# ScalarE in place of GpSimd for the samples' one-hot values, and a later place for the second output gate

## The chip, the cores and the metric

The kernel runs on one core of one Trainium2 chip. The metric is the device time of one execution in microseconds (us); lower is better. Five engines of the core work side by side, each through its own list of instructions in order, and wait for one another through semaphores: TensorE (PE in the profile, its weight loads PEld), VectorE (DVE), ScalarE (ACT), GpSimd (POOL) and SyncE (SP, which here only starts DMA transfers).

## The reference

One layer of a decoder is computed for a prompt (512 tokens) and for 8 samples of 8 new tokens each, 576 tokens in all, model width 1024. An input projection feeds a convolution branch and a matrix-memory branch (mLSTM, 4 heads of width 256); both are gated and merged, and a feed-forward part follows. What matters here is the memory of the samples, which each head updates as

```
C_new = decay[..., None, None] * C + jnp.einsum('bhs,bhsv,bhsk->bhvk', w_s, vc, kc)
...
mlstm_out = (jax.nn.sigmoid(og.astype(jnp.float32)) * hm).astype(x.dtype)
```

For a sample b, the sum over its own 8 tokens s gives a 256x256 matrix from weighted values and keys. `og` is the output gate of the branch.

## The kernel before, in words

Everything is float32 at nearly full precision: TensorE's fast form of float32 (fp32r) is used on split numbers, a high and a low part, so a projection "unit" (one tile of 128 output rows times 576 tokens) is three products: h_hi with w_hi, h_lo with w_hi, h_hi with w_lo. A unit's 128x1024 weights are loaded into `raw` (two slots), ScalarE copies them into `w_hi` (`split_hi`, line 801, called `hi_of` in a head), and VectorE subtracts to get `w_lo` (`split_lo`, line 1689, called `lo_of`, which afterwards runs some taps of the depthwise convolution, line 1911). TensorE runs a unit only once its `w_lo` is there.

The four heads are four turns of one loop on every engine. A head has 10 units: q, k, v, og, gb, two of each. The weights of unit j+2 are split while unit j or j+1 runs: `hi_of(6)` splits the weights of unit 8, `hi_of(7)` those of unit 9. Behind `hi_of(6)` and `hi_of(7)` ScalarE applies a sigmoid with bias to the finished units 6 and 7 and writes the output gate to `merged` (line 967). On VectorE the matching `lo_of(6)` and `lo_of(7)` stand in front of the evaluation of the head's output.

TensorE's order in the second part of a head is: unit 6 with the products of the old states beside it, a small product read by ScalarE (line 1434), unit 7, then the products PV 0 to PV 4 (lines 1449 to 1456, one for each 128 prompt tokens and one for the samples), the prompt's new state (line 1464, two products "CP"), and then unit 8 with eight sample products beside it, one in front of each eighth of the unit (line 1475, "CS 0" to "CS 7", two matmuls each), and unit 9. These results rotate through four PSUM banks; a product may only start when the one four places before it has been read out. So PV 3 waits until ScalarE has copied PV 0 out of PSUM into `num` (line 972), and CS 4 waits until VectorE has read CS 0 and added it to the old state `cs` (line 2015).

The samples' keys and weighted values are stacked by six small DMAs (line 621) into `stk`, in two groups of four samples, each with 96 rows: high, low and high again parts of 4 samples x 8 tokens. For one sample, the values of the others must be zero. So `wvs` holds eight copies of the value block, each multiplied by the sample's column of `oh96`, which is 1 in that sample's rows and 0 elsewhere. GpSimd makes the copies (line 742): one instruction for each group of four samples, 96x1024 elements. It does this behind the eight subtractions that give the low parts of the old states (line 737) and in front of the stores of the states. TensorE waits for `wvs` in front of CS 0.

VectorE's order behind the PV operands is: `w2_lo` (line 1973), `kvn_lo` (line 1977), `lo_of(6)`, `lo_of(7)`, each with two taps, the samples' outputs (lines 1985 to 1993), statistics and small scalars (lines 1997 to 2011), and then CS 0 to CS 7 (line 2015).

Of the kernel before, what the change touches and what calls it, by code (L numbers as in the profile page):

```python
# [27 lines left out]
F32 = mybir.dt.float32  # L28
F32R = mybir.dt.float32r
ALU = mybir.AluOpType  # L30
ACT = mybir.ActivationFunctionType
# [7 lines left out]
SB, SL = 8, 8  # L39
SG = SB // 2  # L40
GT = SG * SL
RING = 3
NH, HD = 4, 256
# [172 lines left out]
def build(nc, xT, vecs, gate_w, gate_b, cache, w_cgcv, w_head, w_ga, w_co, w_o, w_fi, w_fp, w_fo0, w_fo1, w_fo2,  # L216
          st_c, st_n, st_m, y, conv_p, conv_s, cn_p, m_p, c_s, n_s, m_s):
    with ExitStack() as ctx:  # L218
        place = [-(-nc.sbuf_base // 32) * 32]

        def sb(name, cols, dt=F32, parts=P):
            shape = [parts] + (list(cols) if isinstance(cols, (list, tuple)) else [cols])
            t = nc.alloc_sbuf_tensor_at(name, shape, dt, offset=place[0])
            place[0] += -(-4 * int(np.prod(shape[1:])) // 32) * 32
            return t

        def sem(name):
            return ctx.enter_context(nc.semaphore(name))
# [45 lines left out]
        oh96 = sb("oh96", SG)  # L274
# [33 lines left out]
        wvs = nc.alloc_sbuf_tensor_at("wvs", [P, SB, HD], F32R, offset=head_base + 4 * 2 * T)  # L308
# [37 lines left out]
        stk = nc.alloc_sbuf_tensor_at("stk", [P, 2, 2 * HD], F32R, offset=hf_base + 4 * 2 * T)  # L346
# [70 lines left out]
        def slot(s):  # L417
            return ps[:, 2 * s:2 * s + 2, 0:HALF]

        def bank(k):  # L420
            return ps[:, 4 + k % 4, :]
# [14 lines left out]
        def vcol(c, parts=P):  # L436
            return vec[0:parts, c:c + 1] if isinstance(c, int) else vec[0:parts, bass.ds(c, 1)]
# [50 lines left out]
        stk_placed = [sem(f"samples_kv_stacked{g}") for g in range(2)]  # L488
        kvsplit_ready = sem("samples_kv_split")
        wvs_ready = sem("wvs_ready")  # L490
# [166 lines left out]
        def _(pool):  # L657
# [75 lines left out]
            def states(h, last=False):  # L733

                for b in range(SB):
                    pool.wait_ge(cshi_ready, h * SB + (b + 1))
                    pool.tensor_tensor(cs_lo[:, b % RING, :], cs[:, b, :, :].rearrange("p k v -> p (k v)"),  # L737
                                       cs_hi[:, b % RING, :].bitcast(F32), ALU.subtract).then_inc(cslo_ready, 1)

                for g in range(2):  # L740
                    pool.wait_ge(stk_placed[g], h * 48 + 48)
                    pool.tensor_tensor(wvs[0:3 * GT, g * SG:g * SG + SG, :],
                                       stk[0:3 * GT, g, HD:2 * HD].bitcast(F32).unsqueeze(1)
                                       .broadcast_to([3 * GT, SG, HD]),
                                       oh96[0:3 * GT, :].unsqueeze(2).broadcast_to([3 * GT, SG, HD]), ALU.mult)\
                        .then_inc(wvs_ready, 1)

                pool.wait_ge(act_read, h * ACT_USES + (START + ACT_USES))
                pool.dma_start(cn_p[bass.ds(h, 1)].rearrange("o p k v -> (o p) k v"), cp[:, :, :])\
                    .then_inc(cp_stored, 16)  # L750

                pool.wait_ge(dve_read, h * DVE_USES + (START + 13))
                pool.dma_start(c_s[bass.ds(h, 1)].rearrange("o p b k v -> (o p) b k v"), cs[:, :, :, :])\
                    .then_inc(cs_stored, 16)
                pool.wait_ge(cs_stored, h * 16 + 16)
                pool.wait_ge(cp_stored, h * 16 + 16)
                pool.sem_inc(cp_free, 1)
                if not last:
                    pool.dma_start(cs[:, :, :, :], st_c[bass.ds(h + 1, 1)].rearrange("o p b k v -> (o p) b k v"))\
                        .then_inc(cs_loaded, 16)  # L760
# [31 lines left out]
        def _(act):  # L792
# [113 lines left out]
            with act.Fori(0, NH) as h:  # L906
                def hi_of(j):
                    split_hi(h * (PER_HEAD // 2) + (U_B + j + 2) // 2, j % 2)

                def use(k):  # L910
                    act.wait_ge(attn_ready, h * USES + (k + 1))

                for j in range(2):
                    hi_of(j)
                    evac_bias(h, j, halves(qkv[:, 0, :, :], j))
                hi_of(2)

                act.wait_ge(mdiag_ready, h + 1)

                def gcol(item, parts=P):  # L920
                    return cols[0:parts, item, bass.ds(h, 1)]

                for s in range(NB):
                    act.activation(wts[:, W_OFF[s]:W_OFF[s] + P], mdiag[:, s, :], ACT.Exp, bias=gcol(I_G[s]))\
                        .then_inc(w_ready, 1)
                    for t in range(s + 1, NB):
                        o = W_OFF[s] + (t - s) * P
                        act.activation(wts[:, o:o + P], negm[:, bass.ds(h, 1), t * P:t * P + P]
                                       .rearrange("p o n -> p (o n)"), ACT.Exp,
                                       bias=gcol(OFF[s, t])).then_inc(w_ready, 1)  # L930
                act.activation(wts[0:TS, W_OFF[NB]:W_COLS], msamp[0:TS, :], ACT.Exp, bias=gcol(I_G[NB], TS))\
                    .then_inc(w_ready, 1)
                hi_of(3)
                for j in range(4, 6):
                    hi_of(j)
                    evac_bias(h, j, halves(qkv[:, 2, :, :], j - 4))
                def old_hi(b):

                    if b >= RING:
                        act.wait_ge(old_used, h * SB + (b - RING + 1))  # L940
                    act.activation(cs_hi[:, b % RING, :], cs[:, b, :, :].rearrange("p k v -> p (k v)"), ACT.Copy)\  # L941
                        .then_inc(cshi_ready, 1)

                act.wait_ge(cs_loaded, h * 16 + 16)
                for b in range(RING):
                    old_hi(b)
                for i in range(5):
                    use(T_USE + i)
                    n = P if i < NB else TS
                    act.activation(kvn[0:n, i, 0:2 * HD], bank(T_USE + i)[0:n, :], ACT.Copy).then_inc(act_read, 1)  # L950

                for b in range(RING, SB):
                    old_hi(b)

                use(I_USE)
                act.activation(inter_lo[0:TS, :], bank(I_USE)[TS:P, 0:HD], ACT.Copy)
                act.activation(inter[0:TS, :], bank(I_USE)[0:TS, 0:HD + SB], ACT.Copy).then_inc(act_read, 1)

                act.wait_ge(dve_read, h * DVE_USES + (START + 5))
                act.activation(w2_hi[:, :], wts[:, 0:W_OFF[NB]], ACT.Copy).then_inc(pvhi_ready, 1)  # L960
                act.wait_ge(act_read, h * ACT_USES + (START + 5))
                act.activation(v_hi[:, :, :], kvn[:, 0:NB, HD:2 * HD + 2], ACT.Copy).then_inc(pvhi_ready, 1)
                act.wait_ge(out_stored, 16 * 4)
                for j in range(6, 8):
                    hi_of(j)
                    act.wait_ge(unit_done, h * PER_HEAD + (U_B + j + 1))
                    act.activation(halves(merged, h * 2 + (j - 6)), slot(j % 2), ACT.Sigmoid,
                                   bias=vcol(h * PER_HEAD + (U_B + j))).then_inc(slot_read[j % 2], 1)
                for i in range(5):
                    use(PV_USE + i)  # L970
                    n = P if i < NB else TS
                    act.activation(num[0:n, i, :], bank(PV_USE + i)[0:n, 0:VE], ACT.Copy).then_inc(act_read, 1)
                act.wait_ge(cp_free, h + START)
                for k in range(2):
                    use(CP_USE + k)
                    act.activation(cp[:, k, :], bank(CP_USE + k)[:, 0:VE], ACT.Copy).then_inc(act_read, 1)
                act.wait_ge(hvar_ready, h + 1)
                act.activation(small[:, 2, :], small[:, 1, :], ACT.Sqrt, bias=eps[:, :]).then_inc(hdev_ready, 1)
                for j in range(8, 10):
                    hi_of(j)  # L980
                    act.wait_ge(unit_done, h * PER_HEAD + (U_B + j + 1))
                    act.wait_ge(gb_used, h * 2 + START)
                    act.activation(halves(tmp, j % 2), slot(j % 2), ACT.Sigmoid,
                                   bias=vcol(h * PER_HEAD + (U_B + j))).then_inc(slot_read[j % 2], 1)
# [39 lines left out]
            with act.Fori(0, N_CO // 2) as i:  # L1024
                for p in range(2):
                    for o in range(2):
                        j = i * 4 + (2 * p + o)
# [267 lines left out]
        def _(pe):  # L1295
# [71 lines left out]
            with pe.Fori(0, NH) as h:  # L1367
# [99 lines left out]

                for g in range(2):
                    pe.wait_ge(stk_placed[g], h * 48 + 48)
                pe.wait_ge(wvs_ready, h * 2 + 2)  # L1470

                def state_update(b):
                    use(CS_USE + b)
# [1201 lines left out]
```

## Time and profile before

| | us |
|---|---|
| median of 3 runs | 940.04 (939.7 to 940.3) |
| profiled execution | 938.66 |
| span of that execution, first to last instruction | 937.1 |
| TensorE busy in the span | 922.1 (98%) |
| VectorE busy | 777.3 (83%) |
| ScalarE busy | 460.6 (49%) |
| GpSimd busy | 110.5 (12%) |

The page of the profile gives busy time by engine, the groups of instructions with what they waited for, and the DMA issues. The trace behind it can be asked for waits by engine, for the instructions of one line, and for a timeline: start and duration of each instruction of an engine in a window. A row of a timeline merges neighbours of the same line; its duration is from the start of the first to the end of the last. On one engine the start of an instruction may lie a little ahead of the end that is recorded for the one before it, because they overlap.

### The profile page before, as it was taken

How to read it: one execution, taken by the hardware profiler on the slowest of the kernel's cores; microseconds unless marked ns; L12 is line 12 of the kernel's file. 1: busy time of each engine (PE TensorE's matmuls, PEld its weight loads, DVE VectorE, ACT ScalarE, POOL GpSimd, SP SyncE). 2: the span in 40 equal slices, each digit the busy share in tenths (PEclk: the TensorE clock that was granted, in tenths of full speed). 3: DMA queues.
4: the chain of work that ended last, by engine and by line, in shares of the span. 5: the costliest groups of instructions: out<-in, count | busy, mean ns of one | idle time of the engine just before them, and what ended most of it. 6: DMA issues, size and time to landing. Idle time of an engine off the chain costs nothing. (4 is left out here: it accounts for less than half of the span.)

```text
span 937.1 us, 18353 instructions
## 1 busy us (share of the span) xinstructions
PE 922.1 (98%) x6801; PEld 902.0 (96%) x6801; DVE 777.3 (83%) x1227; ACT 460.6 (49%) x676; POOL 110.5 (12%) x109
## 2 busy tenths in 40 slices
PE   8999999999999999999999999999999999999996
PEld 8999999999999999999999999999999999999995
DVE  6899986989698879976355569999888999989997
ACT  7654442444245334524733345456444555456564
POOL 3011330043006001500231000000000000000001
PEclk9999999999999999999999999999999999999999
DMA  6245225211721452142432232232222223233122
GB/s 220 69 155 193 70 74 226 90 55 63 249 88 40 146 179 90 41 167 70 133 125 81 76 90 69 93 125 99 91 90 92 90 72 110 94 117 105 45 91 101
DMA packets 24123, 100.13 MB, mean 107 GB/s; under 512 B 3312, under 2 KB 6529, under 8 KB 19572
## 3 DMA queue, kind: packets, MB, share of 16 engines
q1 hardware_dynamic: 21240, 78.70, 25.5%
q0 software_dynamic: 1984, 19.72, 5.7%
q10 hardware_dynamic: 832, 0.88, 0.3%
q8 instruction: 34, 0.56, 0.2%
q14 instruction: 33, 0.27, 0.1%
HBM read 85.28 MB, written 12.44 MB: 104 GB/s over the span
## 5 line engine op out<-in xcount | busy, mean ns | idle before, releaser
L1306 PE MATMUL ps<-h_hi,w_hi 128*128 128x288 f32 x896 | 193.6, 298 | 0.0
L1306 PE MATMUL ps<-h_lo,w_hi 128*128 128x288 f32 x896 | 191.5, 296 | 0.0
L1306 PE MATMUL ps<-h_hi,w_lo 128*128 128x288 f32 x896 | 191.2, 295 | 0.0
L801 ACT ACTIVATE w_hi<-raw 128x1024 fp32r<-128x1024 f32 x76 | 80.3, 1057 | 171.5 <-PE ps L1306 168.4
L1306 PEld LDWEIGHTS ps<-h_hi,w_lo 128*128 128x128 f32 x896 | 144.2, 189 | 0.0
L1306 PEld LDWEIGHTS ps<-h_hi,w_hi 128*128 128x128 f32 x896 | 143.4, 189 | 0.8
L1306 PEld LDWEIGHTS ps<-h_lo,w_hi 128*128 128x128 f32 x896 | 144.1, 189 | 0.0
L1689 DVE TENSOR_TENSOR w_lo<-raw,w_hi 128x1024 fp32r<-128x1024 f32 x76 | 101.0, 1329 | 47.1 <-ACT w_hi L801 47.1
L1911 DVE SCALAR_TENSOR_TENSOR conv<-a_p,vec,conv x120 | 97.7, 814 | 1.6 <-DVE conv L1911 1.4
L1566 PE MATMUL ps<-cols_b,late 128*128 128x288 f32 x432 | 62.9, 295 | 0.1
L1566 PE MATMUL ps<-cols_a,main 128*128 128x288 f32 x432 | 62.8, 295 | 0.0
L737 POOL TENSOR_TENSOR cs_lo<-cs,cs_hi 128x512 fp32r<-128x512 f32 x32 | 42.4, 1354 | 156.7 <-ACT cs_hi L941 156.7
L1566 PE MATMUL ps<-cols_b,main 128*128 128x288 f32 x432 | 60.2, 295 | 0.2 <-issue 0.2
L1566 PEld LDWEIGHTS ps<-cols_b,late 128*128 128x128 f32 x432 | 59.0, 188 | 0.3 <-issue 0.3
L1566 PEld LDWEIGHTS ps<-cols_a,main 128*128 128x128 f32 x432 | 59.0, 188 | 0.0
L1566 PEld LDWEIGHTS ps<-cols_b,main 128*128 128x128 f32 x432 | 58.2, 188 | 0.4 <-issue 0.4
L1566 PE MATMUL ps<-hid_a,main 128*128 128x288 f32 x396 | 55.3, 296 | 0.5 <-ACT hf L1104 0.5
L788 POOL TENSOR_TENSOR x<-x,rs 128x288 f32<-128x288 f32 x5 | 3.8, 795 | 429.2 <-ACT rs L1272 429.2
L1566 PEld LDWEIGHTS ps<-hid_a,main 128*128 128x128 f32 x396 | 53.3, 188 | 1.0 <-ACT hf L1104 0.7
L1066 ACT ACTIVATE main<-raw 128x1024 fp32r<-128x1024 f32 (+1 forms) x30 | 31.0, 1032 | 34.8 <-PE ps L1566 17.1
L1071 ACT ACTIVATE main<-main 128x1024 fp32r<-128x1024 f32 (+1 forms) x30 | 31.0, 1033 | 32.2 <-DVE main L2171 32.2
L2171 DVE TENSOR_TENSOR main<-raw 128x1024 f32<-128x1024 f32 (+1 forms) x30 | 35.6, 1186 | 7.5 <-PE ps L1566 7.5
(355 smaller groups left out, 1839.6 us busy)
## 6 DMA issues: line engine op xcount, KB each, us to landing
raw<-w_head_in SPq DMA_DIRECT2D x40, 512.0 KB, 3.5
raw<-w_fp_in SPq DMA_DIRECT2D x18, 1024.0 KB, 4.9
cs<-st_c_in POOLq DMA_DIRECT2D x4, 2048.0 KB, 9.3
c_s_out<-cs POOLq DMA_DIRECT2D x4, 2048.0 KB, 7.4
raw<-w_fo_in SPq DMA_DIRECT2D x8, 1024.0 KB, 4.9
x<-xT_in SPq DMA_DIRECT2D x16, 288.0 KB, 4.2
raw<-w_cgcv_in SPq DMA_DIRECT2D x8, 512.0 KB, 3.6
raw<-w_ga_in SPq DMA_DIRECT2D x8, 512.0 KB, 3.5
```

The lines of the kernel that those rows point to most:

```text
L737: pool.tensor_tensor(cs_lo[:, b % RING, :], cs[:, b, :, :].rearrange("p k v -> p (k v)"), cs_hi[:, b % RING, :].bitcast(F32), ALU.subtract ...
L788: pool.tensor_tensor(x[:, k, at], x[:, k, at], rs[:, at], ALU.mult).then_inc(y_pool_ready, 1)
L801: act.activation(w_hi[:, s, :], raw[:, s, :], ACT.Copy).then_inc(hi_ready, 1)
L1066: act.activation(main[:, 0:4:2, 0, 0:n], blocks_of(i)[:, 1:4:2, :], ACT.Copy).then_inc(a11_a12_hi, 1)
L1071: act.activation(main[:, 1:4:2, 0, 0:n], main_32[:, 1:4:2, 1, 0:n], ACT.Copy).then_inc(s1_s3_hi, 1)
L1306: last = pe.matmul(ps[:, 2 * s + b, 0:HALF], wt[:, w, k * P:k * P + P], src[:, k, b * HALF:b * HALF + HALF], start=(k == 0 and wt is w_hi ...
L1566: last = pe.matmul(ps[:, at, 0:HALF], wrows(rows_, wp)[:, k * P:k * P + P], of(cols_, cp_)[:, k, :], start=(first and k == 0 and wp == 0 a ...
L1689: dve.tensor_tensor(w_lo[:, s, :], raw[:, s, :], w_hi[:, s, :].bitcast(F32), ALU.subtract)\
L1911: steps.on(dve.scalar_tensor_tensor(o, a, wcol, o, ALU.mult, ALU.add))
L2171: dve.tensor_tensor(main_32[:, 1:4:2, 1, 0:n], r[:, 0:2, :], r[:, 2, :].unsqueeze(1).broadcast_to([P, 2, n]), ALU.add).then_inc(s1_s3_sum, 1)
```

## The change

GpSimd's two multiplications per head are taken out. ScalarE makes the eight copies instead, one ACTIVATE Copy for each sample, 96x256, with the column of `oh96` as a per-partition scale. They stand behind the first output gate (unit 6) and in front of the five PSUM copies into `num`. The second output gate (`hi_of(7)`, the wait for unit 7 and its sigmoid) is moved from in front of these PSUM copies to behind them. TensorE's wait counts eight copies per head instead of two. VectorE's program stays as it is.

```diff
-                for g in range(2):
-                    pool.wait_ge(stk_placed[g], h * 48 + 48)
-                    pool.tensor_tensor(wvs[0:3 * GT, g * SG:g * SG + SG, :],
-                                       stk[0:3 * GT, g, HD:2 * HD].bitcast(F32).unsqueeze(1)
-                                       .broadcast_to([3 * GT, SG, HD]),
-                                       oh96[0:3 * GT, :].unsqueeze(2).broadcast_to([3 * GT, SG, HD]), ALU.mult)\
-                        .then_inc(wvs_ready, 1)
...
-                for j in range(6, 8):
+                def og_unit(j):
                     hi_of(j)
                     act.wait_ge(unit_done, h * PER_HEAD + (U_B + j + 1))
                     act.activation(halves(merged, h * 2 + (j - 6)), slot(j % 2), ACT.Sigmoid,
                                    bias=vcol(h * PER_HEAD + (U_B + j))).then_inc(slot_read[j % 2], 1)
+
+                og_unit(6)
+                for b in range(SB):
+                    if b % SG == 0:
+                        act.wait_ge(stk_placed[b // SG], h * 48 + 48)
+                    act.activation(wvs[0:3 * GT, b, :], stk[0:3 * GT, b // SG, HD:2 * HD].bitcast(F32),
+                                   ACT.Copy, scale=oh96[0:3 * GT, b % SG:b % SG + 1]).then_inc(wvs_ready, 1)
                 for i in range(5):
                     use(PV_USE + i)
                     n = P if i < NB else TS
                     act.activation(num[0:n, i, :], bank(PV_USE + i)[0:n, 0:VE], ACT.Copy).then_inc(act_read, 1)
+                og_unit(7)
                 act.wait_ge(cp_free, h + START)
...
-                pe.wait_ge(wvs_ready, h * 2 + 2)
+                pe.wait_ge(wvs_ready, h * SB + SB)
```

## Rows read from the trace of the kernel before

**Rows 1.** The page, busy time of each engine and share of the span.
```profile
PE 922.1 (98%) x6801; PEld 902.0 (96%) x6801; DVE 777.3 (83%) x1227; ACT 460.6 (49%) x676; POOL 110.5 (12%) x109
```

**Rows 2.** Waits of TensorE: line waited for, us in total, times, longest.
```profile
PE ps L1475 <- DVE cs L2015: 1.4, 4, 0.4
```

**Rows 3.** Timeline of TensorE: start, us, line, tiles, idle before it.
```profile
139.28 0.42 PE L1306 MATMUL ps<-h_hi,w_lo 128*128 128x288 f32 x2
140.03 0.51 PE L1475 MATMUL ps<-wvs,stk 96*128 96x256 f32 x2 [0.33 <-DVE cs L2015]
...
228.03 0.39 PE L1475 MATMUL ps<-wvs,stk 96*128 96x256 f32 x1 [0.33 <-DVE cs L2015]
```

**Rows 4.** Timeline of VectorE, head 0, from the PV operands to CS 0.
```profile
124.28 2.92 DVE L1977 TENSOR_TENSOR kvn_lo<-kvn,v_hi 128x1024 fp32r<-128x1024 f32 x1
127.12 2.91 DVE L1689 TENSOR_TENSOR w_lo<-raw,w_hi 128x1024 fp32r<-128x1024 f32 x1
...
131.75 1.22 DVE L1689 TENSOR_TENSOR w_lo<-raw,w_hi 128x1024 fp32r<-128x1024 f32 x1
...
139.23 2.06 DVE L2015 SCALAR_TENSOR_TENSOR cs<-cs,dec,ps 128x512 f32<-128x512 f32 x3
```

**Rows 5.** Timeline of ScalarE, head 0, around the output gates.
```profile
124.77 1.28 ACT L967 ACT_TABLE_LOAD   x1
126.06 0.74 ACT L967 ACTIVATE merged<-ps,vec 128x576 f32 x1
127.53 1.06 ACT L801 ACTIVATE w_hi<-raw 128x1024 fp32r<-128x1024 f32 x1 [0.73 <-PE ps L1306]
128.50 0.72 ACT L967 ACTIVATE merged<-ps,vec 128x576 f32 x1
129.12 1.05 ACT L972 ACTIVATE num<-ps 128x257 f32<-128x257 f32 x3
131.37 0.38 ACT L972 ACTIVATE num<-ps 128x257 f32<-128x257 f32 x1 [1.20 <-PE ps L1453]
131.95 0.38 ACT L972 ACTIVATE num<-ps 64x257 f32<-64x257 f32 x1 [0.19 <-PE ps L1456]
133.88 0.39 ACT L976 ACTIVATE cp<-ps 128x257 f32<-128x257 f32 x1 [1.56 <-PE ps L1464]
```

**Rows 6.** Timeline of TensorE where PV 3 starts, and CS 0.
```profile
129.35 0.28 PE L1451 MATMUL ps<-kvn_lo,wts_hi 128*128 128x256 f32 x1
129.47 0.28 PE L1453 MATMUL ps<-v_hi,wts_lo 128*128 128x258 f32 x1
129.62 0.38 PE L1449 MATMUL ps<-v_hi,wts_hi 128*128 128x258 f32 x1
...
135.24 0.59 PE L1475 MATMUL ps<-wvs,stk 96*128 96x256 f32 x2
```

**Rows 7.** Groups by form (busy us, mean ns of one), and two timelines of neighbours.
```profile
L941 ACT ACTIVATE cs_hi<-cs 128x512 fp32r<-128x512 f32 x32 | 19.3, 627 | 9.8 <-PE ps L1426 9.8
L928 ACT ACTIVATE wts<-negm,cols 128x128 f32 x24 | 8.2, 389 | 0.0
...
87.27 0.97 ACT L928 ACTIVATE wts<-negm,cols 128x128 f32 x3
...
9.67 3.66 ACT L810 ACTIVATE xg_hi<-x,vec 128x576 fp32r<-128x576 f32 x5
```

**Rows 8.** Timeline of GpSimd: the two multiplications of head 0.
```profile
123.14 5.82 POOL L742 TENSOR_TENSOR wvs<-stk,oh 96x1024 fp32r<-96x1024 f32 x2 [4.50 <-DMA stk<-kvs]
```

**Rows 9.** VectorE behind a copy of ScalarE, unit 9 of head 0: both timelines.
```profile
151.64 1.06 ACT L801 ACTIVATE w_hi<-raw 128x1024 fp32r<-128x1024 f32 x1 [4.07 <-PE ps L1306]
...
152.73 1.23 DVE L1689 TENSOR_TENSOR w_lo<-raw,w_hi 128x1024 fp32r<-128x1024 f32 x1 [3.59 <-ACT w_hi L801]
```

**Rows 10.** Stretches: busy us and count by engine, then granted clock of TensorE.
```profile
6.00:8.00 2.00, 1.40 (x13) 1.21 (x11) 0.79 (x2) 1.31 (x4) 1.47 (x9) 1.00 1.03 413
158.00:246.00 88.00, 87.67 (x636) 83.79 (x635) 73.98 (x137) 36.93 (x58) 18.23 (x13) 1.00 0.34 115
```

## The prediction

> **What bounds the kernel now.** I read the page first: TensorE is busy for 98% of the span [rows 1], so a change is worth only what it does to TensorE's gaps. The stretches say the same of the heads: one turn of the loop takes 88.00 us and TensorE is busy for 87.67 of them [rows 10]. Next come TensorE's waits. Within the heads one named wait matters, at line 1475 for VectorE's reading of CS 0, four times, once in each head [rows 2]. Then the timelines, to see how this wait arises and how much slack the neighbours have. The heads repeat within hundredths: CS 4 starts at 140.03 in head 0 and at 228.03 in head 1, 88.00 later [rows 3]. So head 0 is worked out and multiplied by four.
>
> Without any wait CS 4 would follow the two matmuls at 139.28 at the usual pace. Neighbouring matmuls start 0.12 us apart [rows 6], so behind those two it would start at about 139.53; it starts at 140.03 [rows 3]. That is a stall of 0.5 us. It ends just after the first CS reading on VectorE, which starts at 139.23. Three readings take 2.06 us [rows 4], so the first is over at about 139.95 and CS 4 starts less than 0.1 later. VectorE reaches 139.23 without an idle stretch from 124.28 on: no row in this stretch has an idle time before it, and those shown lie end to end [rows 4]. Therefore VectorE's chain already sets CS 4, and whatever delays it by one microsecond delays TensorE by one.
>
> ScalarE sets a second, nearly invisible point. PV 3 starts at 129.62, 0.15 behind the matmul at 129.47 where the pace before was 0.12, and its first matmul takes 0.38 instead of 0.28, as after a short wait [rows 6]. ScalarE's copy of PV 0 starts at 129.12 and ends at 129.50 (a copy of this kind takes 0.38) [rows 5]. So PV 3 has no slack left against this copy: it starts 0.12 after its end.
>
> **The change, part by part.**
>
> GpSimd's part. Two multiplications, 5.82 us per head, go away [rows 8]. TensorE needs `wvs` only at CS 0, at 135.24 [rows 6], and it was there at 128.96; so GpSimd's own time was hidden and its removal gives nothing directly. It gives something to VectorE: while GpSimd multiplies, from 123.14 to 128.96, two subtractions of 128x1024 take 2.92 and 2.91 us, while the same subtraction takes 1.22 at 131.75 with GpSimd idle [rows 4, 8]. VectorE so gains 1.70 + 1.69 = 3.4 us and could be at the end of `lo_of(6)` at about 128.3. What is late next is decided below: the weights it needs then are not there.
>
> Where the copies lie. The first output gate starts at 126.06, takes 0.74 and overlaps its successor by about 0.1, so the first copy can start at 126.70 [rows 5]. Its data are there: GpSimd waited for the stacking DMAs only in front of its first multiplication, and began the second, which needs the second group, at about 126.05 [rows 8]. The wait for `stk` that ScalarE gains costs nothing; queued behind it are the `num` copies, for which TensorE waits.
>
> The price of a copy. No 96x256 copy with a scale column is in the trace, so I build it. A plain copy of 512 elements takes 0.627 us [rows 7], one of 1024 takes 1.06 [rows 5]; one element more costs 0.84 ns. Exponentials of 128 elements with a column operand take 0.389 and follow one another by (0.97 - 0.39)/2 = 0.29 [rows 7]. From them: 0.29 + 128 x 0.84 ns = 0.40 per copy. From the only run of copies with a scale column: 3.66/5 = 0.73 at 576 elements, so 0.73 - 320 x 0.84 ns = 0.46 [rows 7]. The lower end is 0.335, the pace of the plain PSUM copies of 257 elements, (1.05 - 0.38)/2, were the column free [rows 5]; the upper one 0.50, the same with no overlap. I take 0.40, as it comes from the row nearest in size.
> The Trainium skill (ScalarE: Activation LUTs, on what an ACTIVATE costs) states that each column operand adds about 93 ns and that neighbours overlap by as much; by its figures an estimate for 256 elements is 0.40 us, so it speaks for the first of the two rows and against the second, and by it the sum stays as below.
>
> First stall, at PV 3. Eight copies are 3.20 us, so they end in time for the PV 0 copy to start at 126.70 + 3.20 = 129.90. Before, `hi_of(7)` and its gate stood there and it started at 129.12. That is +0.78, and with no slack at PV 3 TensorE waits 0.78 us there. The subtraction `kvn_lo` comes earlier, but this buys nothing: what it frees is in front of PV 3, which ScalarE now sets.
>
> Second stall, at CS 4. The last `num` copy (the samples') follows TensorE and so starts at 131.95 + 0.78 = 132.73 [rows 5]. Now `hi_of(7)` comes: it starts 0.29 later (0.38 less the overlap), at 133.02, and takes 1.06, to 134.08. VectorE picks weights up 0.03 after ScalarE's copy ends (151.64 + 1.06 = 152.70, against 152.73) [rows 9]. So `lo_of(7)` starts at 134.11 instead of 131.75: +2.36. VectorE's program is unchanged, so it stands idle from about 128.3, with everything for CS 0 queued behind this one subtraction. From its start to CS 0 VectorE needs 139.23 - 131.75 = 7.48 us without a gap [rows 4]; CS 0 is read from 141.59, and CS 4 starts at 140.03 + 2.36 = 142.39. Of the 2.36 the first stall holds 0.78, this one the other 1.58 on top of the 0.5 that was there.
>
> The rest is covered. The second gate's sigmoid ends at about 134.7, while the first CP copy may now start at 133.88 + 0.78 = 134.66 [rows 5]: it does not move. Between the two gates no other function is loaded: before, a Copy of weights also lay between them with one table load ahead of both [rows 5], so no load is added. Unit 9's weights are ready at 135.3, ten microseconds ahead. After CS 4 VectorE takes under 0.7 us for each reading (2.06/3) [rows 4] and TensorE a microsecond for each eighth of the unit, so no further wait follows. SyncE's next load into this slot is later by 2.4 us and has the better part of a head to spare. GpSimd's stores wait for ScalarE and VectorE as before.
>
> Sum: 4 x 2.36 = 9.4 us. Nothing in the 98% busy TensorE after the heads can give it back. Against the profiled execution: span 937.1 + 9.4 = 946.5, time 938.66 + 9.4 = 948.1. That execution lies 1.4 below the median of the runs shown; from the median, 940.04 + 9.4 = 949.5. That is the forecast.
>
> **The rivals.**
>
> A: the copies are hidden and only the gate's new place counts. If the pause at PV 3 is no wait, or the copies are quicker than 0.30, the `num` copies stay where they are, and `lo_of(7)` starts at 131.95 + 0.29 + 1.06 + 0.03 = 133.33: +1.58 per head, 6.3 in all, 946.4. Against it stand the 0.12 between copy and PV 3 and the price of a copy.
>
> B: a copy costs more. With 0.46 the PV 0 copy starts at 130.38: +1.26, and with the 1.58 that is 2.84 per head, 951.4. With 0.50 and no overlap it is +1.58 and 3.16 per head, 952.7.
>
> C, the other side: VectorE's relief wins. If `lo_of(7)` had its weights by 131.2, the 3.4 us would wipe out the stall of 0.5 at CS 4 (deciding point: CS 0 read 0.5 earlier than now), 4 x 0.5 = 2.0 us: 938.0. It needs `hi_of(7)` ahead of the last `num` copy, and in the new order it lies behind it, while that copy cannot start before 131.95 since it waits for TensorE [rows 5]. The rule behind this is in the Trainium skill (GPSIMD Engine Reference, Key points): GpSimd shares its SBUF interfaces with VectorE and gets in the way of instructions with two SBUF inputs. The trace agrees, by 2.92 against 1.22; it speaks for the change, and only its gain has nowhere to go.
>
> D: the clock. TensorE waits some 2 us in a stretch at CS 4. If its granted clock fell from 2.4 to 1.2 GHz for the four remaining eighths of unit 8 (4.1 us), each head would lose another 4.1: 966. Against it, the clock stays 1.00 in the start-up stretch where TensorE is busy for only 1.40 of 2 us [rows 10]. The Trainium skill (TensorE: Matmul & The Clock Gate) states that a gate halves the clock of an array that is less busy; no row here shows that in mid-kernel.
>
> E: the change cancels out. The bank of PV 3 and the weights of unit 9 would both have to be ready about as early as now; no row offers that, and the chance stands for a reading of mine that is wrong in both places: within 0.2% of 940.04.
>
> **How the numbers follow.** Forecast 0.70, A 0.11, B 0.12, C 0.02, D 0.02, E 0.03. The forecast's own width (copies from 0.335 to 0.42, starts read to 0.05) is about 947.2 to 950.3. The range takes in A and B whole, so 946.0 to 952.8. About 0.2%, 1.9 us, is what a measurement can tell from no change: slower by more 0.95, within 0.03, faster 0.02.
>
> **What would show it.** In the profile after: GpSimd's line gone and the two subtractions at 1.22; eight copies about 0.40 apart; PV 3 waiting for a `num` copy, about 0.8 per head; an idle stretch of VectorE of about 5.8 us per head in front of `lo_of(7)`, released by ScalarE's `w_hi`; TensorE waiting some 2.1 at CS 4, 8 in all; turns of 90.36 us; clock 1.00. It is wrong if `lo_of(7)` starts less than 1.5 us later than now against its head, or if VectorE's 7.48 us from there to CS 0 shrinks.

## The result and the profile of the changed kernel

The change makes the kernel slower. The median is 952.62 us (951.71 to 954.4, 4 runs) against 939.87 before (939.7 to 940.3, 4 runs); the ratio is 1.0137 with a 95% interval of 1.012 to 1.0155. The profiled execution took 953.48 us with a span of 952.0. On the page of the changed kernel, the busy times, which answer to [rows 1], and the granted clock in 40 slices:

```profile
PE 929.0 (98%) x6801; PEld 908.3 (95%) x6801; DVE 764.6 (80%) x1227; ACT 472.4 (50%) x708; POOL 86.3 (9%) x101
...
PEclk9999999999999999999999999999999999999998
```

GpSimd has lost 24 us, VectorE 13, and TensorE's share is 98% as before: the page alone doesn't show what went wrong. TensorE's waits do (line waited for, us in total, times, longest), beside [rows 2]:

```profile
PE ps L1475 <- DVE cs L2015: 7.6, 4, 1.9
PE ps L1449 <- ACT num L971: 3.1, 4, 0.8
```

These are the two predicted waits, in front of CS 4 and of PV 3, in every head. (The 1.9 is TensorE's idle time by the row; counted from the time at which CS 4 would have started at the usual pace, as the prediction counts, it is 2.1.) In this kernel line 971 is the `num` copy, 966 the value copies, 959 the output gate, 793 the weight copy. The timeline of ScalarE in head 0, beside [rows 5]. The whole head lies 0.58 us later than before, since the start-up of this execution was slower: the row `inter_lo` starts at 121.48 here and at 120.90 before.

```profile
121.48 0.38 ACT L948 ACTIVATE inter_lo<-ps 64x256 f32<-64x256 f32 x1 [4.29 <-PE ps L1434]
...
126.64 0.74 ACT L959 ACTIVATE merged<-ps,vec 128x576 f32 x1
127.28 3.30 ACT L966 ACTIVATE wvs<-stk,oh 96x256 fp32r<-96x256 f32 x8
130.47 0.91 ACT L971 ACTIVATE num<-ps 128x257 f32<-128x257 f32 x3
...
133.29 0.38 ACT L971 ACTIVATE num<-ps 64x257 f32<-64x257 f32 x1 [0.19 <-PE ps L1456]
133.57 1.04 ACT L793 ACTIVATE w_hi<-raw 128x1024 fp32r<-128x1024 f32 x1
```

The eight copies run from 127.28 to the first `num` copy at 130.47, 0.40 us apart. VectorE in the same head, beside [rows 4]:

```profile
124.86 1.22 DVE L1977 TENSOR_TENSOR kvn_lo<-kvn,v_hi 128x1024 fp32r<-128x1024 f32 x1
125.99 1.22 DVE L1689 TENSOR_TENSOR w_lo<-raw,w_hi 128x1024 fp32r<-128x1024 f32 x1
...
134.65 1.23 DVE L1689 TENSOR_TENSOR w_lo<-raw,w_hi 128x1024 fp32r<-128x1024 f32 x1 [5.64 <-ACT w_hi L793]
...
142.14 4.04 DVE L2015 SCALAR_TENSOR_TENSOR cs<-cs,dec,ps 128x512 f32<-128x512 f32 x6
```

Both subtractions take 1.22 instead of 2.92 and 2.91, and VectorE then stands idle for 5.64 us until the weights of unit 9 have been copied. From there to CS 0 it is 142.14 - 134.65 = 7.49 us, as before. On TensorE, head 0 and then heads 1 to 3, beside [rows 3, 6]:

```profile
130.97 0.38 PE L1449 MATMUL ps<-v_hi,wts_hi 128*128 128x258 f32 x1 [0.78 <-ACT num L971]
...
142.94 0.50 PE L1475 MATMUL ps<-wvs,stk 96*128 96x256 f32 x2 [1.90 <-DVE cs L2015]
...
233.28 0.70 PE L1475 MATMUL ps<-wvs,stk 96*128 96x256 f32 x2 [1.90 <-DVE cs L2015]
...
325.13 0.51 PE L1475 MATMUL ps<-wvs,stk 96*128 96x256 f32 x2 [1.90 <-DVE cs L2015]
...
417.03 0.51 PE L1475 MATMUL ps<-wvs,stk 96*128 96x256 f32 x2 [1.90 <-DVE cs L2015]
```

Less the 0.58, CS 4 of head 0 is at 142.36; 142.39 was forecast. From head 0 to head 1 a turn takes 90.34 us, and 90.36 was forecast. But the next two turns take 91.85 and 91.90. The stretches of head 1 show why (us; busy us and count by engine; the eighth number, behind POOL's count, is the granted clock as a share of full speed):

```profile
230.00:232.00 2.00, 1.38 (x11) 1.15 (x9) 1.79 (x11) 0.00 (x0) 0.00 (x0) 1.00 0.09 35
232.00:233.60 1.60, 0.32 (x2) 0.33 (x3) 1.49 (x5) 0.30 (x1) 0.00 (x0) 0.94 0.00 0
233.60:234.00 0.40, 0.40 (x3) 0.40 (x3) 0.40 (x2) 0.00 (x0) 0.00 (x0) 0.50 0.00 0
234.00:236.00 2.00, 2.00 (x10) 2.00 (x10) 1.86 (x4) 0.00 (x0) 0.00 (x0) 0.50 0.00 0
236.00:237.00 1.00, 1.00 (x7) 1.00 (x6) 0.74 (x1) 0.00 (x0) 0.00 (x0) 0.59 0.00 0
237.00:240.00 3.00, 3.00 (x24) 2.82 (x23) 1.63 (x4) 0.78 (x1) 0.05 (x1) 1.00 0.00 0
```

Behind the wait at CS 4 the granted clock falls from 2.4 to 1.2 GHz and is back at about 236.8; from the shares 0.94 and 0.59 it was low from about 233.4, for 3.4 us. The rows of TensorE show it too: a pair of matmuls of unit 8 takes 0.68 us in that time and 0.42 after it.

```profile
233.77 0.68 PE L1306 MATMUL ps<-h_hi,w_hi 128*128 128x288 f32 x2
...
237.22 0.42 PE L1306 MATMUL ps<-h_hi,w_hi 128*128 128x288 f32 x2
```

A turn with such a fall is 91.87 - 90.34 = 1.53 us longer. In this execution heads 1, 2 and 3 have one, head 0 has none.

So the 14.9 us between the two spans are: 0.58 from the start, 4 x 2.34 = 9.4 from the two waits, 3 x 1.53 = 4.6 from the clock, and 0.3 not assigned.

### The profile page after: what moved, and what is told of

The parts are those of the page before. It is cut to its first block and busy times, and to the rows that moved or that the text cites. A ratio compares the mean times of both kernels' runs of the same rounds, so it can differ in the third digit from the quotient of the medians.

```text
span 952.0 us, 18378 instructions
## 1 busy us (share of the span) xinstructions
PE 929.0 (98%) x6801; PEld 908.3 (95%) x6801; DVE 764.6 (80%) x1227; ACT 472.4 (50%) x708; POOL 86.3 (9%) x101
## 5 line engine op out<-in xcount | busy, mean ns | idle before, releaser
L1689 DVE TENSOR_TENSOR w_lo<-raw,w_hi 128x1024 fp32r<-128x1024 f32 x76 | 94.3, 1241 | 69.8 <-ACT w_hi L793 69.8
L1911 DVE SCALAR_TENSOR_TENSOR conv<-a_s,vec,conv x120 | 41.7, 348 | 0.0
```

What stands on the lines that cost most here:

```text
L1689: dve.tensor_tensor(w_lo[:, s, :], raw[:, s, :], w_hi[:, s, :].bitcast(F32), ALU.subtract)\
L1911: steps.on(dve.scalar_tensor_tensor(o, a, wcol, o, ALU.mult, ALU.add))
```

## The experiments

Two theories go through the expectations. W: the waits at PV 3 and CS 4 are all that the change brings, and what lies beyond their 9.4 us has another cause. W+C: the long wait also brings the clock down, which costs the rest. The experiments first split the change, then take the two waits and the fall apart, then build a version without either. The kernel before ran beside them: 938.69 us (15 runs) beside the first four, 939.66 (24 runs) beside the last four.

**The gate's new place alone.** The value copies stay on GpSimd (edit against the kernel before).

```diff
-                for j in range(6, 8):
-                    hi_of(j)
...
+                og_unit(6)
                 for i in range(5):
                     use(PV_USE + i)
...
+                og_unit(7)
```

> Only the second output gate is moved behind the num copies; GpSimd still makes the values. Theory W+C (waits, plus a fall of TensorE's clock behind the long wait): no wait at PV 3, lo_of(7) later by 1.55 us, CS 4 waits 2.05 us instead of 0.5, so +6.2 us, and the granted clock falls to 1.2 GHz for about 3.4 us behind CS 4 in up to all four heads, 1.7 us each: 946.1 plus 1.7 for each fall, up to 952.9. Theory W (the 3.5 us beyond the waits in the changed kernel come from something else, such as the copies on ScalarE): 946.1, clock as before. If the fall needs both waits of a head, also 946.1.

Measured: 946.67 us (945.56 to 947.79, 4 runs), ratio 1.0081 (1.0065 to 1.0096). TensorE's waits have the one at CS 4 and none at PV 3. The stretches of the four heads:

```profile
PE ps L1478 <- DVE cs L2018: 7.6, 4, 1.9
...
70.00:158.00 88.00, 86.10 (x621) 82.27 (x620) 76.19 (x141) 38.14 (x60) 21.57 (x19) 0.98 0.36 122
158.00:246.00 88.00, 86.10 (x625) 82.28 (x624) 72.93 (x136) 37.04 (x58) 18.03 (x13) 1.00 0.33 115
246.00:334.00 88.00, 86.10 (x626) 82.38 (x624) 73.17 (x137) 36.03 (x57) 17.97 (x13) 1.00 0.33 111
334.00:422.00 88.00, 86.10 (x612) 82.44 (x612) 74.36 (x137) 36.35 (x58) 18.27 (x13) 0.98 0.31 108
```

The gate's move alone makes the long wait, and the clock falls in two of the four heads. From head 0 to head 3 three turns take 269.70 us (`inter_lo` from 120.87 to 390.57), 5.7 more than before; with one fall of 1.5 among them that leaves 1.4 per head, where 1.55 was expected. The missing 0.15 is the small wait at PV 3 in the kernel before: with ScalarE free, the `num` copies follow TensorE, PV 3 starts without it, and against its head the samples' `num` copy comes 0.14 earlier than before. The total is 4 x 1.4 + 2 x 1.5 = 8.6 by this count, and 8.0 was measured between the medians; the four runs differ in their mean clock (0.992 to 0.996), so they need not all have two falls.

**The copies alone.** The second gate stays in front of the `num` copies, behind the value copies.

```diff
                 og_unit(6)
                 for b in range(SB):
...
+                og_unit(7)
                 for i in range(5):
                     use(PV_USE + i)
...
-                og_unit(7)
```

> ScalarE makes the copies, the second gate stays in front of the num copies (behind the value copies). Both theories: PV 3 waits 2.4 us for the PV 0 copy, which comes 3.20 us of copies later less the 0.8 us that ScalarE idled there; VectorE gets its weights for unit 9 in time and is held only by the last num copy, so CS 4 has no wait: +2.4 - 0.5 = 1.9 per head, 947.6. Theory W+C adds 1.7 us for each head in which the clock falls behind the single 2.4 us wait (947.6 to 954.4); theory W adds nothing. If VectorE's relief from GpSimd did not count, CS 4 would still wait 0.5 and the time be 949.6.

Measured: 955.47 us (953.11 to 956.55, 4 runs), ratio 1.0171 (1.0155 to 1.0187). One part alone is at least as slow as both together: the ratio lies above the changed kernel's 1.0137, and just above the 1.0149 of its second measurement (last experiment), whose interval this one overlaps. Waits and stretches of the four heads:

```profile
PE ps L1449 <- ACT num L972: 9.4, 4, 2.4
...
70.00:158.00 88.00, 85.65 (x601) 81.17 (x600) 71.40 (x138) 39.63 (x67) 15.08 (x16) 0.96 0.35 115
158.00:246.00 88.00, 85.65 (x612) 81.71 (x611) 71.00 (x137) 39.57 (x66) 12.21 (x11) 0.98 0.30 103
246.00:334.00 88.00, 85.65 (x600) 81.06 (x600) 67.24 (x128) 36.80 (x63) 11.65 (x10) 0.96 0.31 103
334.00:422.00 88.00, 85.65 (x611) 81.57 (x611) 69.11 (x134) 39.88 (x66) 12.18 (x11) 0.98 0.34 115
```

The wait has moved whole to PV 3, 2.4 us in one piece, and the one at CS 4 is gone, as expected. The clock falls in all four heads, and in two of them it stays low about twice as long (a share of 0.04 instead of 0.02 is missing). The time lies 16.8 us above the kernel before. The waits explain 7.7 at most (a turn with one fall takes 91.20 us, which less 1.5 is 1.7 above 88.00, where 1.9 was expected), the clock the rest. This is more than the upper end that was expected: one fall for each head was assumed, not one that lasts twice as long.

**The wait filled with work.** The changed kernel; in front of CS 4, TensorE multiplies into an unused part of a PSUM bank. The results are read by nobody.

```diff
                 def state_update(b):
+                    if b == 4:
+                        for _ in range(20):
+                            pe.matmul(ps[:, 2, HALF:512], h_hi[:, 0, 0:P], h_hi[:, 0, 0:512 - HALF],
+                                      start=True, stop=True)
                     use(CS_USE + b)
```

> The changed kernel with 20 matmuls of 224 columns in front of TensorE's wait at CS 4, into a part of a PSUM bank that nobody uses: about 2 us of work in which TensorE waited 2.06 us. Theory W+C: the waits stay as long, but TensorE does not stand idle, the granted clock stays 1.00, and of the changed kernel's 952.6 only the waits' 9.3 us remain: 949.3. Theory W: no change from 952.6.

Measured: 948.82 us (947.27 to 950.69, 4 runs), ratio 1.0106 (1.009 to 1.0122), 10.1 us above the kernel before beside it, where the changed kernel was 12.8 and, measured again, 13.4 above. The filler, and a head's stretch:

```profile
140.64 2.39 PE L1475 MATMUL ps<-h_hi 128*128 128x224 f32 x20
142.87 0.41 PE L1479 MATMUL ps<-wvs,stk 96*128 96x256 f32 x2
...
158.00:246.00 88.00, 87.22 (x639) 83.56 (x637) 68.55 (x136) 39.40 (x66) 11.65 (x10) 1.00 0.32 111
```

CS 4 is at least as late as in the changed kernel (142.87 - 0.33 for the later start = 142.54, against 142.36), but the clock is 1.00 in all four heads, and every turn takes 90.41 us, as the changed kernel's turn without a fall (90.34). Added work that nobody needs makes the kernel faster: the intervals of the two ratios only touch (1.0122 here, 1.012 there), the turns leave no doubt. This is what tells W from W+C: the copies on ScalarE, the DMAs and the waits of VectorE are all as in the changed kernel; only TensorE's idleness is taken away. Of the 0.8 us above the expected 9.3, 4 x 0.07 = 0.3 is the filler itself, 2.39 us long where 2.06 were free.

**The subtraction behind two CS readings.** The changed kernel; on VectorE, unit 9's `w_lo` no longer stands in front of CS 0.

```diff
                 lo_of(6)
-                lo_of(7)
+                taps(7)
...
                 for b in range(SB):
+                    if b == 2:
+                        split_lo(h * PER_HEAD + (U_B + 7 + 2), 1)
                     use(CS_USE + b)
```

> The changed kernel, but on VectorE the subtraction of unit 9's weights goes behind the second CS reading (its two taps stay in front). Theory W+C: what delayed CS 4 was only that CS 0 was queued behind this subtraction. CS 0 is now held by the last num copy and is read well before CS 4 needs it; the wait at CS 4 goes (against 2.06 us), PV 3 still waits 0.8 us, and such a wait does not bring the clock down: 4 x (0.8 - 0.5) = +1.2 us against the kernel before, about 939.9 beside 938.7, granted clock 1.00 throughout the heads. Rival: the clock falls also behind the short wait at PV 3: up to 1.7 us more per head, up to 946.7. Rival: CS 4 is held by something else: above 944.

Measured: 940.28 us (939.14 to 941.24, 10 runs), ratio 1.0005 (0.9996 to 1.0015), so no difference from the kernel before can be told. Waits of TensorE, VectorE's new order, one head's stretch:

```profile
PE ps L1449 <- ACT num L971: 3.1, 4, 0.8
...
137.75 1.41 DVE L2017 SCALAR_TENSOR_TENSOR cs<-cs,dec,ps 128x512 f32<-128x512 f32 x2
139.07 1.22 DVE L1689 TENSOR_TENSOR w_lo<-raw,w_hi 128x1024 fp32r<-128x1024 f32 x1
...
158.00:246.00 88.00, 87.22 (x635) 83.55 (x635) 71.02 (x137) 39.90 (x66) 12.21 (x11) 1.00 0.34 115
```

The wait at CS 4 is gone from the list, so what held it was the queue behind the subtraction. PV 3 waits 0.8 us as before this edit, and behind that wait the clock does not fall, in no head. The time rises by 0.6 us, a little under the expected 1.2, within what the measurement can tell.

**The copies behind the num copies.** GpSimd's part is gone, the second gate is in its old place, and TensorE waits for each sample's copy by itself.

```diff
                 og_unit(6)
+                og_unit(7)
+                for i in range(5):
+                    use(PV_USE + i)
...
                 for b in range(SB):
                     if b % SG == 0:
                         act.wait_ge(stk_placed[b // SG], h * 48 + 48)
...
-                for i in range(5):
-                    use(PV_USE + i)
...
-                og_unit(7)
...
-                pe.wait_ge(wvs_ready, h * SB + SB)
                 def state_update(b):
                     use(CS_USE + b)
+                    pe.wait_ge(wvs_ready, h * SB + (b + 1))
```

> ScalarE makes the copies, but behind the num copies, with the second gate in its old place, and TensorE waits for each sample's copy on its own. Theory: ScalarE is free from 132.3 to 133.9, the first copy is there before CS 0 at 135.2 and each next one is 0.40 us later against 1.03 us on TensorE; the first CP copy comes about 1.6 us later, which CS 2 does not feel. VectorE has 3.4 us back, CS 0 is read as soon as TensorE has made it, and the 0.5 us wait at CS 4 goes: -0.5 x 4 = -2.0, 937.9, clock unchanged. Rival: VectorE's relief buys nothing: 939.9. Rival: the later CP copies make CS 2 or CS 3 wait: above 940.5.

Measured: 936.48 us (935.42 to 937.96, 11 runs), ratio 0.9976 (0.9967 to 0.9985). It beats both kernels, and it did so again beside the last group:

> The late copies once more, beside the idle products: -2.2 us against the kernel before, as the first time (0.9976).

Measured: 936.78 us (936.38 to 937.62, 8 runs), ratio 0.9969 (0.9959 to 0.998). The copies on ScalarE in the first of these kernels, TensorE around CS 4, and one head:

```profile
132.41 3.29 ACT L971 ACTIVATE wvs<-stk,oh 96x256 fp32r<-96x256 f32 x8
...
139.48 0.42 PE L1306 MATMUL ps<-h_hi,w_lo 128*128 128x288 f32 x2
139.73 0.40 PE L1475 MATMUL ps<-wvs,stk 96*128 96x256 f32 x2
...
158.00:246.00 88.00, 87.99 (x641) 84.32 (x640) 71.39 (x137) 39.80 (x66) 12.20 (x11) 1.00 0.35 119
```

The same eight copies at the same price now fill a time in which ScalarE waited for TensorE anyway. CS 4 follows its neighbours at the usual pace, and TensorE is busy for 87.99 of 88.00 us, where it was 87.67 [rows 10]. Three turns take 262.2 us instead of 264.0, 0.6 less per head; 0.5 was expected.

**Idle products on GpSimd.** The late copies, and GpSimd multiplies the same amount as before into a spare tile, for which TensorE waits in front of CS 0. The spare tile is half as large, so it does so in four instructions of 96x512. Nothing reads their results.

```diff
+                for g in range(2):
+                    pool.wait_ge(stk_placed[g], h * 48 + 48)
+                    for part in range(2):
...
+                        pool.tensor_tensor(spare[0:3 * GT, :, :],
+                                           stk[0:3 * GT, g, HD:2 * HD].bitcast(F32).unsqueeze(1)
+                                           .broadcast_to([3 * GT, SG // 2, HD]),
+                                           oh96[0:3 * GT, 2 * part:2 * part + 2].unsqueeze(2)
+                                           .broadcast_to([3 * GT, SG // 2, HD]), ALU.mult)\
+                            .then_inc(spare_ready, 1)
...
+                pe.wait_ge(spare_ready, h * 4 + 4)
```

> The kernel with the late copies, in which GpSimd also multiplies the same 2048 elements per partition and head as before, into a spare tile that nobody reads (in four instructions instead of two); TensorE waits for them before CS 0, as before. Theory: what the late copies gained was VectorE's relief from GpSimd. Two subtractions take 2.9 us again, CS 0 is read 3.4 us later, CS 4 waits 0.5 us again: 938.7, as the kernel before. Rival: the gain has another source (the copies made one by one, or the wait per sample): it stays at 936.5.

Measured: 939.11 us (937.82 to 939.81, 11 runs), ratio 0.9993 (0.9984 to 1.0002), 2.3 us above the late copies beside it. VectorE and GpSimd:

```profile
124.41 2.06 DVE L1992 TENSOR_TENSOR kvn_lo<-kvn,v_hi 128x1024 fp32r<-128x1024 f32 x1
126.39 2.06 DVE L1704 TENSOR_TENSOR w_lo<-raw,w_hi 128x1024 fp32r<-128x1024 f32 x1
128.38 1.52 DVE L1926 SCALAR_TENSOR_TENSOR conv<-a_p,vec,conv  x1
...
123.28 7.52 POOL L747 TENSOR_TENSOR spare<-stk,oh 96x512 f32<-96x512 f32 x4 [4.50 <-DMA stk<-kvs]
...
123.28 2.11 POOL L747 TENSOR_TENSOR spare<-stk,oh 96x512 f32<-96x512 f32 x1 [4.50 <-DMA stk<-kvs]
125.47 1.90 POOL L747 TENSOR_TENSOR spare<-stk,oh 96x512 f32<-96x512 f32 x1
```

With GpSimd busy most of the gain of the late copies is gone, though the wait per sample and the single copies are still there; so it was VectorE's relief. A turn takes 87.77 us, against 87.39 with the late copies and 88.00 before. What is left of the gain fits VectorE too: against its head it reads CS 0 still 0.21 us earlier than before (139.14 - 121.02, against 139.23 - 120.90).

The subtractions take 2.06 and not 2.9, and a tap is slowed as well (1.52 where it took 0.74). The ends of the rows show a pattern that neither the prediction nor the expectation had. The two subtractions end at 126.47 and 128.45, each 1.08 us behind the end of the GpSimd instruction in which it started (125.39 and 127.37). In the kernel before they end at 127.20 and 130.03, again 1.08 behind the ends of GpSimd's two multiplications (126.12 and 128.95), and the other heads of both profiles agree within 0.02. Alone a subtraction takes 1.22. So VectorE seems to have stood until GpSimd's current instruction was over and then to have run at its usual pace; half as long instructions on GpSimd then cost less each. No run was made to test this reading.

**The changed kernel again**, on the chip of the last group and without any edit.

> The changed kernel as it is, beside the others on one chip. Theory W+C: 938.7 + 9.3 for the waits, plus 1.7 for each head behind whose wait at CS 4 the clock falls, two to four of them: 951.4 to 954.8. If the falls were an accident of the first runs: 948.

Measured: 953.05 us (952.63 to 954.52, 4 runs), ratio 1.0149 (1.0134 to 1.0165). In its profile the stretches of heads 0, 1 and 3 have a clock of 0.98, that of head 2 has 1.00. The falls come again, three of four, but not in the same heads.

## Why the prediction was right, and where it was not

The direction and the mechanism of the waits were right, and the time lies inside the range. That it does is in part luck. The likeliest value, 949.5, was 3.1 us too low, because a term was put at nothing; the range reached up to 952.8 only for the sake of dearer copies (rival B), which did not come, and 952.62 lies 0.2 below that end. Two of the four runs lie above it, and so does the median of the second measurement, 953.05. Step by step:

- *GpSimd's time was hidden; its removal relieves VectorE by 3.4 us.* Right: 1.22 and 1.22 us for the two subtractions. That this relief had nowhere to go in the changed order, and only there, is shown by the late copies (-2.2 and -2.9) and by the idle products, which take most of it back. So rival C was right in its mechanism and priced well (2.0); what decided was the place, as the prediction said.
- *A copy costs 0.40 us.* Right: (130.47 - 127.28)/8 = 0.40. One takes 0.50. The price from the run with the scale column, 0.46, was too high, so rival B falls; the Trainium skill's figures (ScalarE: Activation LUTs, What ACT_TABLE_LOAD costs) gave an estimate of 0.40 too.
- *PV 3 has no slack, and the wait is 0.78.* Right: 0.78 in the row of PV 3. That it waited already before, by some 0.14, is shown by the gate moved alone, where the `num` copies have ScalarE to themselves and CS 4 came that much earlier than expected. Rival A falls. But the reason given ahead of the prediction, that a product waits for the one four places before it, doesn't fit here: PV 0 is only three places in front of PV 3. In the kernel the wait that belongs to the samples' product, PV 4, stands one product early, in front of PV 3 (`if k + 1 in samples and k >= 3: read(k - 3)`). So the 0.78 us hang on the place of a wait; PV 3's own bank had been read long before. Whether they would go with the wait moved behind PV 3 was not tested.
- *`lo_of(7)` comes 2.36 later and CS 4 with it.* Right: `lo_of(7)` came 134.65 - 131.75 - 0.58 = 2.32 later and CS 4 142.94 - 140.03 - 0.58 = 2.33 later in head 0, and the first turn took 90.34. The subtraction behind two CS readings shows that the queue on VectorE was the cause.
- *The clock stays at 1.00.* This is the step that failed. Rival D had the mechanism, with a chance of 0.02, and two mistakes. Its price was too high: a fall lasts 3.4 us and costs 1.5, not 4.1. And its chance was far too low. The row that was brought against it was the start-up stretch, where TensorE was busy for 1.40 of 2 us at a clock of 1.00. That stretch cuts a wait in two, which is 1.29 us long as a whole (first line below); the one at issue is 1.90. So the row says nothing about a wait half as long again. And the trace of the kernel before does hold a fall, at its end, behind the last matmul (second line, a clock of 0.75). With the price right, three falls are 4.6 us. Then the profiled execution should take 948.1 + 0.6 for its start + 4.6 = 953.3, and it took 953.48. Without them the forecast of 9.4 above the kernel before fits the filled kernel, 10.1.

```profile
8.69 0.37 PE L1333 MATMUL ps<-xg_hi,gstat 128*128 128x288 f32 x1 [1.29 <-ACT gstat L816]
...
930.00:937.10 7.10, 0.00 (x0) 0.00 (x0) 2.62 (x7) 0.28 (x1) 2.97 (x4) 0.75 0.90 314
```

So the term of the sum that was missing is the clock. It also decides which half of the change was worse. In waits alone, the copies cost 1.7 to 1.9 us per head (2.4 at PV 3 less the 0.5 or 0.6 that goes at CS 4), the gate's place 1.4, and both together 2.34. They do not add up. This is read from the rows and no run of its own shows it: with the gate behind the `num` copies, the value copies fill a time in which ScalarE would otherwise be idle in front of PV 0, and only their rest of 0.78 is late.

## What to carry to other kernels

In a kernel that is 98% busy on one engine, every gap of that engine is on the path, and small gaps show where a neighbour has no slack left: a start 0.12 us behind the end of a copy is such a sign, even where the profile names no wait. Ahead of moving work to an engine with low total load, look at what stands behind it in that engine's queue. ScalarE was 49% busy, and the same eight copies cost 1.9 us per head in one place and nothing in another, a few instructions further down. And a wait of some 2 us on TensorE is to be priced with the clock that may fall behind it, not by its own length.

## What the runs showed of the hardware that was not expected

The granted clock falls from 2.4 to 1.2 GHz in the middle of a busy kernel, behind a single wait. TensorE had stood idle for 1.9 us in front of CS 4 (or 2.35 us in front of PV 3) and was busy without a gap worth naming on both sides of it, but for the 0.8 us at PV 3. In all twelve falls of the profiles the clock went down 0.05 to 1.5 us behind the end of the wait, so with TensorE busy again; it was low for 3.4 us, in two cases twice that, and rose again with TensorE busy all along. It isn't certain: three of four heads in two profiles of the changed kernel, two of four with the gate alone, four of four with the longer wait, and other heads each time. It was never seen behind idle times of 0.3 or 0.8 us (the kernel before, and with the subtraction moved), behind the 1.3 us at the start-up of the kernel before, nor where the wait at CS 4 was filled with matmuls.

The runs without a profile agree. Their mean clock over the whole execution is 0.989 to 0.992 in all eight runs of the changed kernel and 0.984 to 0.987 in the four with the copies alone; it is 0.994 or more in the 39 runs of the kernel before beside the experiments and in the four of the filled one.

The Trainium skill (TensorE: Matmul & The Clock Gate, What's actually happening) says that the clock follows how busy the array has been, and in its section HAM oscillation it describes a kernel that swings between the two levels through a wait on DMA in each tile. The runs agree with the direction; here a single wait for VectorE is enough, and its price is 1.5 us.

Why the clock stays high in some heads after the same wait was not tested and stays open.
